# Second block's attention by pairs of heads, laid between the k-tiles of its projections

## The chip, the cores and the metric

The kernel runs on one core of a Trainium2 chip. The metric is the time of one execution in microseconds (us), median of 3 runs. The engines meet at semaphores: TensorE (PE in the rows, PEld its weight loads), VectorE (DVE), ScalarE (ACT), GpSimd (POOL) and SyncE (SP), which issues the weight transfers.

## The reference, cut to what matters

Two transformer blocks over 256 tokens of width 2048, in float32, one after the other. The change is in the attention half of the second:

```
u = rmsnorm_2(h, norm_attn[l])
p = jnp.split(u @ w_in[l], offsets, axis=-1)          # 2048 -> 4224 columns
o_mla = mla_mixer(...)   # 8 heads, latent q and kv, keys of 64+32, causal
o_fox = fox_mixer(...)   # 8 heads of 64, causal, forget-gate bias added to scores
o_nsa = nsa_mixer(...)   # 8 heads of 64 over 2 key groups: compressed, selected, window
o_swa = swa_mixer(...)   # 8 heads of 64 over 2 key groups, window 128, sinks
o = concatenate(...); o = rmsnorm_2(o per group of 512); h = h + o @ w_out[l]
```

Each attention is softmax(q k^T scale + bias) v. NSA's three branches are three softmaxes of the same queries, weighted by gates and added. The compressed branch has only 15 keys. An MLP follows (2048 to 8192 and back).

## The kernel before, in words

Activations lie transposed: 128 features on the partitions by 256 tokens, 16 k-tiles for 2048 features. A weight comes from memory in slots of 2048 columns (1 MB) into a ring of four (`ring`). ScalarE rounds each slot to a high part (`w_high`, L922) and VectorE subtracts to get the low part (`w_low`, L1394), both in two halves, into a pair of buffers. TensorE makes three products of high and low parts (float32r) for each k-tile: L484 to L486 where the weight is stationary ("wide"), L498 to L500 where the activation is ("tall"). Small products (queries from the latent, compression, scores, values) are plain float32 matmuls, which the trace records as two instructions each; transposes are recorded as one.

Every engine runs an order written out by hand. In the second block it is: the norm `attn2`; then the nine groups of `w_in_2` without a break (`group3` for `mla_c, fq, fk, fv, nq, nk, nv, sq`, then `small`), where the groups before `small` are 512 columns wide but for `nv` (384) and have four slots each; then, alone on TensorE, compression (L805, 64x64 pieces with 15 columns), the latent's norm (L652) and its products (L824, L830, L840, L492); then `attention("2")`; then the norm `group` and the product with `w_out_2`.

`attention("2")` runs 48 units, six for each of 8 heads: FOX, SWA, MLA, and NSA's three branches. For unit i TensorE does `score(i)` (L692, for FOX also L696 and L697 with 8 rows), then `turn(i-2)` (L711, three transposes) and `value(i-3)` (L722). VectorE scales the scores and adds the bias (L1501), takes the row maximum (L1512) and later divides by the row sum (L1535). ScalarE does the exponentials with their row sums (L1024), copies the turned probabilities out of PSUM (L1035) and the result (L1042). A head has 64 rows of contraction in its scores (96 in MLA) and 64 columns of output in its values, so one unit's matmuls use half of the array's rows or columns. The slots of `wout2` are split after the last unit.

SP's queue issues the slots in the order of `STREAM`. A slot is loaded again when its four-slots-older one is split, or, for a slot that TensorE reads raw, when its product is done.

## Time and profile before

| | us |
|---|---|
| median of 3 runs | 2594.13 |
| the runs | 2580.07 to 2596.78 |
| the profiled execution, its own time | 2572.51 |
| its span in the profile | 2570.3 |
| dense groups of `w_in_2` (in the span) | 1303 to 1494 |
| compression and latent products | 1494 to 1562 |
| `attention("2")` | 1562 to 1719 |
| norm `group` to the steady part of `wout2` | 1719 to 1745 |

Over the whole span TensorE is busy 94%, its weight loads 78%, VectorE 53%, ScalarE 38%. Matmuls overlap one another in the records, so the distance from start to start says what one costs, not its length. "PEclk" and the granted clock say which share of 2.4 GHz TensorE was given; it has two levels, 2.4 GHz (1.00) and 1.2 GHz (0.50), and a mean between them is a mix.

### The profile page before, as it was taken

What the parts mean: (1) busy time and instruction counts of PE and PEld (TensorE: products, weight loads), DVE (VectorE), ACT (ScalarE), POOL (GpSimd) and SP (SyncE); (2) the same over time, 40 slices, a digit from 0 to 9 for tenths busy, and PEclk for the clock granted to TensorE, in tenths of its full rate; (3) what the DMA queues carried; (4) which work ended last, traced back from release to release, by engine and by line L of the source; (5) the groups of instructions that cost most, each with busy time, mean ns of one, the idle gap of its engine ahead of it and who ended that gap; (6) DMA issues with size and microseconds to landing.
All of it is one profiled execution on the core that took longest, in us unless ns stands there. A gap on an engine that the chain in (4) does not pass through costs nothing.

```text
span 2570.3 us, 31240 instructions
## 1 busy us (share of the span) xinstructions
PE 2412.4 (94%) x12470; PEld 1998.0 (78%) x12470; DVE 1359.2 (53%) x1628; ACT 979.5 (38%) x1299; POOL 160.1 (6%) x61
## 2 busy tenths in 40 slices
PE   6988996998999999999989988979999999999997
PEld 5866565877888888888789975547888888888886
DVE  5388736464555554444554424665655555544444
ACT  4211105352434444444433424553534343444443
POOL 0388310000000000000000000000000000000000
PEclk9999998999999999999999977789999999999999
DMA  6433361549666655565535511004556665555552
GB/s 234 133 113 100 130 151 49 173 132 203 204 186 189 192 184 196 194 238 190 178 127 182 189 54 45 1 34 144 166 182 187 188 192 186 193 190 189 193 196 82
DMA packets 147777, 404.23 MB, mean 157 GB/s; under 512 B 14961, under 2 KB 22385, under 8 KB 126449
## 3 DMA queue, kind: packets, MB, share of 16 engines
q1 hardware_dynamic: 133056, 385.51, 45.5%
q10 hardware_dynamic: 14640, 17.61, 3.2%
q8 instruction: 56, 0.92, 0.1%
q14 instruction: 25, 0.20, 0.0%
HBM read 396.80 MB, written 6.29 MB: 157 GB/s over the span
## 4 chain that ended last, share of the span: by engine, by line
PE 83%; DVE 11%; ACT 3%; DMA 2%; issue 1%; ACTq 0%; DVEq 0%; SPq 0%
PE ps L569 17%; PE ps L605 11%; PE ps L607 11%; PE ps L606 11%; PE ps L570 9%; PE ps L476 3%; PE ps L492 2%; PE ps L484 2%; PE ps L486 2%; PE ps L485 2%; PE ps L692 2%; PE ps L722 2%; DVE scratch L1282 2%; DVE w_low L1394 2%; DMA raw_weights<-in_w_ff 1%; DVE scratch L1660 1%
## 5 line engine op out<-in xcount | busy, mean ns | idle before, releaser
L1394 DVE TENSOR_TENSOR w_low<-raw_weights,w_high 128x1024 fp32r<-128x1024 f32 (+1 forms) x660 | 776.3, 1218 | 902.1 <-ACT w_high L922 902.1
L922 ACT ACTIVATE w_high<-raw_weights 128x1024 fp32r<-128x1024 f32 (+1 forms) x660 | 660.4, 1049 | 900.5 <-PE ps L607 502.4
L569 PE MATMUL ps<-x_split,w_high 128*128 128x512 f32 x2048 | 719.9, 396 | 10.9 <-DVE w_low L1394 8.4
L570 PE MATMUL ps<-x_split,w_low 128*128 128x256 f32 x2048 | 573.8, 280 | 0.0
L605 PE MATMUL ps<-w_high,x_split 128*128 128x512 f32 x1280 | 499.9, 391 | 30.5 <-DVE x_split L1282 27.4
L606 PE MATMUL ps<-w_low,x_split 128*128 128x512 f32 x1280 | 499.1, 390 | 0.0
L607 PE MATMUL ps<-w_high,x_split 128*128 128x512 f32 x1280 | 499.0, 390 | 0.0
L569 PEld LDWEIGHTS ps<-x_split,w_high 128*128 128x128 f32 x2048 | 386.5, 189 | 101.3 <-DVE w_low L1394 8.4
L570 PEld LDWEIGHTS ps<-x_split,w_low 128*128 128x128 f32 x2048 | 389.2, 190 | 0.0
L605 PEld LDWEIGHTS ps<-w_high,x_split 128*128 128x128 f32 x1280 | 241.0, 188 | 82.1 <-DVE x_split L1282 28.1
L607 PEld LDWEIGHTS ps<-w_high,x_split 128*128 128x128 f32 x1280 | 240.9, 188 | 50.4
L606 PEld LDWEIGHTS ps<-w_low,x_split 128*128 128x128 f32 x1280 | 241.1, 188 | 49.9
L476 PE MATMUL ps<-x_over_high,raw_weights 128*128 128x256 f32 x768 | 170.0, 382 | 0.5
L476 PEld LDWEIGHTS ps<-x_over_high,raw_weights 128*128 128x128 f32 x768 | 145.4, 191 | 25.5 <-issue 3.3
L484 PE MATMUL ps<-x_split,w_high 128*128 128x256 f32 x416 | 118.8, 286 | 7.5 <-issue 7.2
L485 PE MATMUL ps<-x_split,w_high 128*128 128x256 f32 x416 | 118.6, 285 | 0.0
L486 PE MATMUL ps<-x_split,w_low 128*128 128x256 f32 x416 | 118.5, 285 | 0.0
L939 ACT ACTIVATE region<-ps 128x1024 f32<-128x1024 f32 (+4 forms) x20 | 18.0, 901 | 206.3 <-PE ps L476 111.1
L484 PEld LDWEIGHTS ps<-x_split,w_high 128*128 128x128 f32 x416 | 80.8, 194 | 8.1 <-issue 8.0
L1024 ACT ACTIVATE scratch<-scratch,small_stats 128x128 f32<-128x128 f32 (+2 forms) x120 | 52.3, 437 | 80.7 <-DVE small_stats L1512 64.9
L485 PEld LDWEIGHTS ps<-x_split,w_high 128*128 128x128 f32 x416 | 80.8, 194 | 0.0
L486 PEld LDWEIGHTS ps<-x_split,w_low 128*128 128x128 f32 x416 | 80.7, 194 | 0.0
(221 smaller groups left out, 2013.4 us busy)
## 6 DMA issues: line engine op xcount, KB each, us to landing
raw_weights<-in_w_ff SPq DMA_DIRECT2D x128, 1024.0 KB, 5.2
raw_weights<-in_w_up SPq DMA_DIRECT2D x64, 1024.0 KB, 5.3
raw_weights<-in_w_down SPq DMA_DIRECT2D x64, 1024.0 KB, 4.9
raw_weights<-in_w_in SPq DMA_DIRECT2D x62, 1024.0 KB, 5.4
raw_weights<-in_w_out SPq DMA_DIRECT2D x32, 1024.0 KB, 4.9
raw_weights<-in_w_mem_kv SPq DMA_DIRECT2D x8, 1024.0 KB, 7.3
t_table<-region ACTq DMA_DIRECT2D x1, 4096.0 KB, 46.0
region<-t_table ACTq DMA_DIRECT2D x1, 3072.0 KB, 18.0
```

Of the source, the lines that this page charges most:

```text
L476: last = nc.tensor.matmul(acc[:, c], w[:, P * c:P * c + P], x, start=(kt == 0 and c % 2 == 0), stop=(kt == kts - 1), skip_group_check=True)
L484: nc.tensor.matmul(o, h, xh_, start=(first and c % 2 == 0), stop=False, skip_group_check=True)
L485: nc.tensor.matmul(o, h, xl_, start=False, stop=False, skip_group_check=True)
L486: last = nc.tensor.matmul(o, wl[:, P * c:P * c + P], xh_, start=False, stop=done, skip_group_check=True)
L569: nc.tensor.matmul(o, wh[:, q, w], xs[:, kt], start=(kt == 0), stop=False, skip_group_check=True)
L570: last = nc.tensor.matmul(o[:, 0:S], wl[:, q, w], xh[:, kt], start=False, stop=(kt == KT - 1), skip_group_check=True)
L605: nc.tensor.matmul(o, h, wh[:, r], start=(first and j == 0), stop=False, skip_group_check=True)
L606: nc.tensor.matmul(o, h, wl[:, r], start=False, stop=False, skip_group_check=True)
L607: last = nc.tensor.matmul(o, l, wh[:, r], start=False, stop=True, skip_group_check=True)
L922: nc.scalar.activation(split_slot(wh_t, k)[:, r], ring_slot(n)[:, r], ACT.Copy).then_inc(rounded, 1)
L1024: last = nc.scalar.activation(s, s, ACT.Exp, bias=nmax[:, r, t:t + 1], accum_out=psumr[:, r, t:t + 1])
L1394: V.tensor_tensor(split_slot(wl_t, k)[:, r], ring_slot(n)[:, r], split_slot(wh_t, k)[:, r].bitcast(f32), ALU.subtract).then_inc(split_read ...
```

## The change

The order of the second block's attention half is rewritten on all engines.

- **Pairs.** The 48 units of one head become 24 duos of two heads (`duo`): 4 of MLA, 12 of NSA, 4 of SWA, 4 of FOX, in this order. The heads of a pair lie on different halves: `ACROSS` pairs a head of key group 0 with one of key group 1, so their scores contract over partitions 0 to 63 and 64 to 127; `EVEN` pairs an even head with an odd one. Values of the two go to output partitions 0 to 63 and 64 to 127. VectorE and ScalarE handle both heads in one instruction where shapes allow. NSA's branches no longer add up in PSUM: each is copied to `mix`, and VectorE adds them (`branches`).
- **Weaving.** `duo_step(p)` (values of p-3, turns of p-2, scores of p) is called between k-tiles of the last five groups: `sq`, `fq`, `fk`, `fva`, `fvb` (`fv` is cut into two groups of 256 columns). `WOVEN` says how many duos go to each slot: eight slots have two, eight have one. The latent's products are called between k-tiles of `nv`, compression between those of `nq`. Only the turns and values of the last duos stand after the last group.
- **Halves.** In the woven part ScalarE and VectorE split the next slot by halves, one half to a duo (both to one, where the slot has one). `wout2`'s first slots are split before the group norm.
- Groups, their slots and their PSUM buffers stand in a new order, `small` first; other buffers moved with them.

```diff
-W2_GROUPS = ("mla_c", "fq", "fk", "fv", "nq", "nk", "nv", "sq")
-STREAM += [(g, 4, True, 1) for g in W2_GROUPS]
-STREAM += [("small", 2, True, 1), ("cmpk", 1, False, 1), ("cmpk2", 0, False, 1), ("cmpv", 1, False, 1), ("cmpv2", 0, False, 1),
-           ("uqa", 1, False, 1), ("uqar", 0, False, 1), ("uqb", 1, False, 1), ("uqbr", 0, False, 1), ("kper", 0, False, 1),
-           ("kna", 0, False, 1), ("knb", 0, False, 1), ("mv", 1, False, 1),
+STREAM += [("small", 2, True, 0), ("mla_c", 4, True, 0), ("nk", 4, True, 0), ("uqa", 1, False, 0), ("uqb", 1, False, 0),
+           ("nv", 4, True, 0), ("ukv", 1, False, 0), ("cmpk", 1, False, 0), ("cmpv", 1, False, 0), ("nq", 4, True, 0),
...
+        EVEN = [(2 * i, 2 * i + 1) for i in range(4)]
+        ACROSS = [(0, 5), (1, 4), (2, 7), (3, 6)]
...
+        DENSE2 = ("small", "mla_c", "nk", "nv", "nq", "sq", "fq", "fk", "fva", "fvb")
+        WOVEN = {"sq": (2, 2, 1, 2), "fq": (2, 1, 2, 2), "fk": (1, 2, 2, 1), "fva": (1, 1), "fvb": (1, 1)}
+        WOVEN_SLOTS = [(g, j) for g in WOVEN for j in range(len(WOVEN[g]))]
+        AHEAD = WOVEN_SLOTS[1:] + [("wout2", 0)]
...
+            def duo_scores(p):
+                x = duos[p]
+                n = x["n"]
+                for t, _, w in KEYS2:
+                    w = min(w, n)
+                    o = [ps[:, 4 + a, n * t:n * t + w] for a in range(2)]
+                    for a in range(2):
+                        last = nc.tensor.matmul(o[a], x["q"][a][:, P * t:P * t + P], x["k"][a][:, 0:w], start=True, stop=not x["extra"])
+                    if x["extra"]:
+                        rows = [slice(64 * a, 64 * a + 8) for a in range(2)]
+                        col = [ident[64 * a:64 * a + 8, 64 * a + h:64 * a + h + 1] for a, h in enumerate(x["heads"])]
+                        for a in range(2):
+                            nc.tensor.matmul(o[a], fc8[rows[a], P * t:P * t + P], col[a].to_broadcast([8, w]), start=False, stop=False)
+                        for a in range(2):
+                            last = nc.tensor.matmul(o[a], col[a].to_broadcast([8, P]), fneg[rows[a], 0:w], start=False, stop=True)
+                m.did(last, "scores2", p)
+            def duo_turn(p):
+                x = duos[p]
+                n = x["n"]
+                w = min(P, n)
+                for a in range(2):
+                    for kt, t, c in turns_of(x):
+                        k0 = (KEYS2[t][1] if n == S else n * t) + P * kt
+                        last = nc.tensor.transpose(ps[0:w, 6 + a, c:c + P], prob2[:, p % 2, a, k0:k0 + w], ident[:, :])
+                m.did(last, "turned2", p)
+            def duo_value(p):
+                x = duos[p]
+                w = min(P, x["n"])
+                turns = turns_of(x)
+                for kt, t, c in turns:
+                    for a, h in enumerate(x["heads"]):
+                        o = ps[x["base"][a]:x["base"][a] + 64, 6 + t, 384:512]
+                        last = nc.tensor.matmul(o, x["v"](kt, h), probT2[0:w, a, c:c + P], start=(kt == 0),
+                                                stop=((kt + 1, t) not in [(u[0], u[1]) for u in turns]), skip_group_check=True)
+                m.did(last, "value2", p)
+            def duo_step(p):
+                if 0 < p < ND:
+                    pe.wait_ge(dve_done, at("scaled2", p - 1))
+                elif 0 <= p - 2 < ND:
+                    pe.wait_ge(dve_done, at("probs2", p - 2))
+                if p >= 4:
+                    pe.wait_ge(act_done, at("out2", p - 4))
+                elif p == 3:
+                    pe.wait_ge(act_done, at("probT2", 0))
+                if p >= 3 and p - 3 == ND - 1:
+                    pe.wait_ge(act_done, at("probT2", p - 3))
+                for first, group_name in ((SWA0, "sq"), (FOX0, "fk"), (FOX0 + 3, "fva"), (FOX0 + 5, "fvb")):
+                    if p == first:
+                        pe.wait_ge(act_done, at("evac", group_name))
+                if 0 <= p - 3 < ND:
+                    duo_value(p - 3)
+                if 0 <= p - 2 < ND:
+                    duo_turn(p - 2)
+                if p < ND:
+                    duo_scores(p)
...
+            def dense(name, form="wide", width=512, sk=SK, after=None):
+                b = DENSE2.index(name)
+                if b >= 2:
+                    pe.wait_ge(act_done, at("evac", DENSE2[b - 2]))
+                for j in range(KT // sk):
+                    k = SPLIT_OF[SLOT0[name] + j]
+                    wh, wl = (split_slot(t, k)[:, 0:sk * width].rearrange("p (k c) -> p k c", k=sk) for t in (wh_t, wl_t))
+                    for q in range(sk):
+                        kt = sk * j + q
+                        if q % (sk // 2) == 0:
+                            pe.wait_ge(split_ready, 2 * k + 1 + q // (sk // 2))
+                        if b == 0 and kt % 4 == 0:
+                            pe.wait_ge(dve_done, at("attn2", "out", kt // 4))
+                        a = (wh[:, q], wl[:, q], xh[:, kt], xl[:, kt], kt == 0, kt == KT - 1)
+                        last = wide3(pair4(b % 2), *a, cols=width // P) if form == "wide" else tall3(pair(b % 2), *a, n=width)
+                        if q == sk - 1:
+                            last.then_inc(split_used, 1)
+                        if after is not None:
+                            after(kt)
...
+            def latent(kt):
+                if kt == 0:
+                    pe.wait_ge(dve_done, at("mlan", "out"))
+                    pe.wait_ge(blk2_loaded, 80)
+                    queries(0)
+                if kt == 2:
+                    queries(1)
+                if kt == 4:
+                    queries_turned(0)
+                if kt == 6:
+                    queries_turned(1)
+                if kt == 8:
+                    keys(0)
+                if kt == 10:
+                    keys(1)
...
+            def compressed(kt):
+                if kt < 8:
+                    compress(kt // 4, kt % 4)
...
+            dense("small", width=256, sk=8)
+            dense("mla_c")
+            dense("nk", after=latent_sums)
+            dense("nv", "tall", 384, after=latent)
+            dense("nq", after=compressed)
             pe.wait_ge(dve_done, at("ready2"))
-            pe.wait_ge(act_done, at("evac", "mv"))
-            attention("2")
+            pe.wait_ge(act_done, at("evac", "cmpv2"))
+            for g in WOVEN:
+                def duos_after(kt, g=g):
+                    sk = KT // len(WOVEN[g])
+                    j, q = kt // sk, kt % sk
+                    ticks = TICKS[g, j]
+                    if len(ticks) == 2 and q in (0, 2):
+                        duo_step(ticks[q // 2])
+                    if len(ticks) == 1 and q == sk // 2 - 1:
+                        duo_step(ticks[0])
+                if g in ("fva", "fvb"):
+                    dense(g, "tall", 256, 8, after=duos_after)
+                else:
+                    dense(g, after=duos_after)
+            for p in range(TAIL0, ND + 3):
+                duo_step(p)
...
+            for (g, j), (nxt, q) in zip(WOVEN_SLOTS, AHEAD):
+                ticks = TICKS[g, j]
+                for c, p in enumerate(ticks):
+                    if c == 0 and j == 0 and g in DONE_BY:
+                        done = DONE_BY[g]
+                        if done == "fq":
+                            act.wait_ge(pe_done, at("scores2", NSA0 - 1))
+                        evac2(done, *homes[done])
+                    duo_back(p)
+                    for h in (c,) if len(ticks) == 2 else (0, 1):
+                        round_half(nxt, q, h)
+                    duo_exps(p)
...
+            def low_half(name, j, h):
+                n, k = SLOT0[name] + j, SPLIT0[name] + j
+                dve.wait_ge(rounded, 2 * k + h + 1)
+                r = slice(HALF * h, HALF * (h + 1))
+                V.tensor_tensor(split_slot(wl_t, k)[:, r], ring_slot(n)[:, r], split_slot(wh_t, k)[:, r].bitcast(f32),
+                                ALU.subtract).then_inc(split_ready, 1)
...
+            def duo_scale(p, negsink):
+                x, r = duos[p], p % 2
+                n = x["n"]
+                dve.wait_ge(pe_done, at("scores2", p))
+                m.own()
+                by_t = lambda a: a.rearrange("p (t k) -> p t k", k=n)
+                if n == S:
+                    for t, k0, w in KEYS2:
+                        ins = V.scalar_tensor_tensor(prob2[:, r, :, k0:k0 + w], ps[:, 4:6, S * t:S * t + w], x["scale"], x["biases"][t],
+                                                     ALU.mult, ALU.add)
+                        m.did(ins, "scaled2", p)
...
+            def duo_normal(p):
+                x, r = duos[p], p % 2
+                n = x["n"]
+                dve.wait_ge(act_done, at("exp2", p))
+                if x["sink"]:
+                    tt(psumr2[:, r], psumr2[:, r], esink2[:, r], ALU.add)
+                    m.own()
+                m.did(V.reciprocal(pinv2[:, r], psumr2[:, r]))
+                m.own()
+                if x["gate"] is not None:
+                    i, j = (8 + 3 * h + x["gate"] for h in x["heads"])
+                    tt(pinv2[:, r], pinv2[:, r], gates[:, :, i:j + 1:j - i], ALU.mult)
+                    m.own()
+                if n == S:
+                    for t, k0, w in KEYS2:
+                        e = prob2[:, r, :, k0:k0 + w]
+                        tt(e, e, pinv2[:, r, t].unsqueeze(2).to_broadcast([P, 2, w]), ALU.mult, "probs2", p)
...
+            for (g, j), (nxt, q) in zip(WOVEN_SLOTS, AHEAD):
+                ticks = TICKS[g, j]
+                for c, p in enumerate(ticks):
+                    duo_scale(p, rinv[:, S:S + 8])
+                    branches(p)
+                    for h in (c,) if len(ticks) == 2 else (0, 1):
+                        low_half(nxt, q, h)
+                    duo_normal(p)
```

On TensorE, in the first woven group but one step (program order; L539 to L541 are the three products of a k-tile's 128 columns, L811 values, L800 transposes, L782 scores). Before, where attention begins:

```order
L492 MATMUL ps<-raw_weights,mixed 128x512 x2
L849 MATMUL ps<-ident,region 128x32 x2
L692 MATMUL ps<-region 128x128
L696 MATMUL ps<-ident,region 128x128
L697 MATMUL ps<-region,ident 128x128
L692 MATMUL ps<-region 128x256
L696 MATMUL ps<-ident,region 128x256
L697 MATMUL ps<-region,ident 128x256
L692 MATMUL ps<-region 128x128
L692 MATMUL ps<-region 128x256
```

And now, at one of the first NSA duos:

```order
L541 MATMUL ps<-x_split,w_low 128x256
L811 MATMUL ps<-region 64x128 x6
L800 MATMUL ps<-ident,region 128x128 x6
L782 MATMUL ps<-region 128x128 x2
L782 MATMUL ps<-region 128x256 x2
L539 MATMUL ps<-x_split,w_high 128x256
L540 MATMUL ps<-x_split,w_high 128x256
L541 MATMUL ps<-x_split,w_low 128x256
```

Before, a unit follows a unit and no dense product stands near. Now a step of 12 + 4 program matmuls for two heads stands between k-tiles of 12 dense ones; two k-tiles (24 dense matmuls) lie between steps where a slot has two duos, four where it has one.

On VectorE, one unit before (L1501 scale, L1512 maximum, L1535 division):

```order
L1501 SCALAR_TENSOR_TENSOR scratch<-ps,region 128x128
L1501 SCALAR_TENSOR_TENSOR scratch<-ps,region 128x256
L1512 TENSOR_REDUCE small_stats<-scratch 128x1 x2
L1527 RECIPROCAL small_stats<-small_stats 128x2
L1282 TENSOR_TENSOR small_stats<-small_stats,region 128x2
L1535 TENSOR_SCALAR scratch<-scratch,small_stats 128x128
L1535 TENSOR_SCALAR scratch<-scratch,small_stats 128x256
```

One duo now (L1776 scale, L1787 maximum, L1764 half a slot's low part, L1521 division):

```order
L1776 SCALAR_TENSOR_TENSOR region<-ps,region 128x2x128
L1776 SCALAR_TENSOR_TENSOR region<-ps,region 128x2x256
L1787 TENSOR_REDUCE small_stats<-region 128x2 x2
L1764 TENSOR_TENSOR w_low<-raw_weights,w_high 128x1024
L1804 RECIPROCAL small_stats<-small_stats 128x4
L1521 TENSOR_TENSOR small_stats<-small_stats,region 128x4
L1521 TENSOR_TENSOR region<-region,small_stats 128x2x128
L1521 TENSOR_TENSOR region<-region,small_stats 128x2x256
```

The division of a duo now follows its own maximum, with half a slot between. Before, the next unit's scale and maximum came first: the reciprocal and what follows in the excerpt above belong to the unit before the one just scaled.

## Rows read from the trace of the kernel before

**Rows 1.** The page: span, busy time, granted clock in 40 slices of the span

```profile
span 2570.3 us, 31240 instructions
PE 2412.4 (94%) x12470; PEld 1998.0 (78%) x12470; DVE 1359.2 (53%) x1628; ACT 979.5 (38%) x1299; POOL 160.1 (6%) x61
...
PEclk9999998999999999999999977789999999999999
```

**Rows 2.** Windows: stretch, busy us (instructions) by engine, clock, DMA share, GB/s

```profile
1340.00:1360.00 20.00, 20.00 (x169) 20.00 (x169) 8.28 (x8) 9.15 (x10) 0.00 (x0) 1.00 0.55 176
1303.00:1494.00 191.00, 190.57 (x1441) 186.35 (x1441) 82.00 (x78) 74.54 (x84) 0.00 (x0) 0.99 0.54 170
1494.00:1523.00 29.00, 24.36 (x262) 23.70 (x262) 2.17 (x11) 4.64 (x16) 0.00 (x0) 0.58 0.12 34
1523.00:1562.00 39.00, 25.90 (x89) 15.51 (x90) 17.36 (x24) 16.41 (x26) 0.00 (x0) 0.88 0.25 91
1562.00:1719.00 157.00, 148.22 (x568) 87.68 (x568) 88.12 (x360) 76.28 (x281) 0.00 (x0) 0.74 0.01 2
```

**Rows 3.** Waits of 1562 to 1719: who for whom, us, times, longest

```profile
DVE scratch L1501 <- PE ps L692: 33.1, 31, 2.8
DVE scratch L1501 <- PE ps L697: 25.4, 8, 4.9
```

**Rows 4.** Windows within attention: busy TensorE at either clock

```profile
1585.80:1589.20 3.40, 3.40 (x10) 1.66 (x10) 2.02 (x8) 1.28 (x6) 0.00 (x0) 0.50 0.00 0
...
1616.40:1619.80 3.40, 3.40 (x19) 2.02 (x17) 2.23 (x10) 1.99 (x9) 0.00 (x0) 1.00 0.01 2
```

**Rows 5.** Timeline of TensorE in attention at full clock: start us, us, instruction

```profile
1597.45 0.92 PE L692 MATMUL ps<-region 64*128 64x128 f32 x4
1598.30 0.55 PE L711 MATMUL ps<-ident,scratch 128*128 128x128 f32 x3
1598.78 0.86 PE L722 MATMUL ps<-scratch,region 128*64 128x256 f32 x4
...
1602.46 0.49 PE L692 MATMUL ps<-region 64*128 64x128 f32 x2
...
1605.90 0.48 PE L711 MATMUL ps<-ident,scratch 128*128 128x128 f32 x1
```

**Rows 6.** Timeline of TensorE in the first block: tiles of 32 between projections

```profile
315.94 1.48 PE L675 MATMUL ps<-scratch,region 128*32 128x256 f32 x24
317.34 1.98 PE L492 MATMUL ps<-raw_weights,x_over_high 128*128 128x512 f32 x4
319.26 2.36 PE L666 MATMUL ps<-region 32*128 32x256 f32 x16
```

**Rows 7.** The chain of waits: float32 projection, and the splits before `moments`

```profile
87.27 27.63 PE ps L476 x128
...
1723.17 2.88 DVE w_low L1394 x3
```

**Rows 8.** Timeline of TensorE: compression begins

```profile
1493.99 9.65 PE L805 MATMUL ps<-region,raw_weights 64*64 64x15 f32 x128
```

**Rows 9.** Timeline of VectorE in one unit of attention

```profile
1627.47 0.62 DVE L1501 SCALAR_TENSOR_TENSOR scratch<-ps,region 128x128 f32<-128x128 f32 x2 [0.91 <-PE ps L692]
1628.12 0.61 DVE L1512 TENSOR_REDUCE small_stats<-scratch 128x1 f32<-128x128 f32 x2
...
1629.10 0.55 DVE L1535 TENSOR_SCALAR scratch<-scratch,small_stats 128x128 f32<-128x128 f32 x2
```

**Rows 10.** Timeline of ScalarE: a unit's two exponentials, then a copy

```profile
1625.74 0.40 ACT L1024 ACTIVATE scratch<-scratch,small_stats 128x128 f32<-128x128 f32 x1 [2.98 <-DVE small_stats L1512]
...
1626.63 0.36 ACT L1042 ACTIVATE mixed<-ps 64x256 f32<-64x256 f32 x1
1626.89 0.47 ACT L1035 ACTIVATE scratch<-ps 128x384 f32<-128x384 f32 x1
```

**Rows 11.** The page, costliest groups: the splits

```profile
L1394 DVE TENSOR_TENSOR w_low<-raw_weights,w_high 128x1024 fp32r<-128x1024 f32 (+1 forms) x660 | 776.3, 1218 | 902.1 <-ACT w_high L922 902.1
L922 ACT ACTIVATE w_high<-raw_weights 128x1024 fp32r<-128x1024 f32 (+1 forms) x660 | 660.4, 1049 | 900.5 <-PE ps L607 502.4
```

More of the change, by code:

```diff
@@ new lines, in compress @@
+            def compress(b, part):
+                name = ("cmpk", "cmpv")[b]
+                if part == 0:
+                    pe.wait_ge(dve_done, at("kcp", b))
+                    pe.wait_ge(act_done, at(*(("gates",) if b else ("evac", "mv"))))
+                w = raw(name).rearrange("p (l c) -> p l c", l=CMP_LEN)
+                for l in range(8 * part, 8 * part + 8):
+                    for g in range(2):
+                        r = slice(64 * g, 64 * g + 64)
+                        last = nc.tensor.matmul(pair(3 - b)[r, g, 0:NCMP], w[r, l], kcp[b][r, l], start=(l == 0), stop=(l == CMP_LEN - 1))
+                if part == 3:
+                    m.did(last, "slot", SLOT0[name])
+                    book["acc", name] = m.n
@@ L1718, in _ @@
             down("ff2_1", up("ff1_1", "mlp", t5_mask))
-            low("mla_c", 0)
+            low("small", 0)
             row_sums("mpost", "ff2_1")
```

645 lines of the change are left out of this document (351 added, 294 removed).

## The prediction

> **What bounds the kernel now.** I read the page first: TensorE is busy 94% of the span and the clock falls from 9 tenths to 7 only in four slices, about 1480 to 1735 us [rows 1]. The windows cut that region by stage [rows 2]. The dense groups run at clock 0.99 with TensorE never idle: 169 matmuls of 256 columns in 20 us, 118 ns each. Compression and latent products take 68 us (29 at clock 0.58, 39 with TensorE busy 25.90). Attention takes 157 us with TensorE busy 148.22, no weight loading, and a clock of 0.74. The waits say who ends last in attention: VectorE waits for scores 58.5 us in all [rows 3], so TensorE is the bound there, and it is slow for two reasons: each matmul uses half of the rows or columns, and the clock is at 1.2 GHz about half of the time. The second isn't idleness: two equal windows have TensorE busy 3.40 of 3.40 us, one at 0.50 and one at 1.00 [rows 4].
>
> The sum is made against the profiled execution, 2572.5 us (span 2570.3). The three timed runs stood 8 to 24 us above it (median 2594.1). I take 15 of that for the median.
>
> **The change, part by part.**
>
> *Compression and latent products* move between k-tiles of `nq` and `nv`. Nothing is removed, so their TensorE time at full clock remains: a 256-column float32 instruction costs 27.63/128 = 216 ns [rows 7], so queries 48 x 0.216 = 10.4, keys 16 x 0.216 = 3.5, sums 8 x 0.216 = 1.7, and 12 instructions of 512 columns (rotation, values) 12 x 0.43 = 5.2; the gates' transposes 0.5. Compression is 256 instructions at 9.65/128 = 75 ns [rows 8]; they now alternate between two quarters of the array. Bounds: 256 x 75 = 19 us if nothing overlaps, half of that, 10, if all does. I take 14. Sum 35. The stage cost 68, most of it chains of copy and wait that the k-tiles now cover: between two calls lie two k-tiles of `nv` or one of `nq`. Where cover fails: `nq`'s third and fourth slot can be loaded only when compression has read its two raw slots, and a load and a split then lie before k-tiles 8 and 12; and the last small chain (gelu, copy, `ready2`) ends about with `nq`. For this 4 us. Net 68 - 39 = **29 saved**.
>
> *Scores, transposes, values* per duo at full clock. In one unit, start to start: scores 0.85 (4 instructions), transposes 0.48 (3), values 0.80 to 0.86 [rows 5]. A pair's scores on different row halves: between 0.85 (both at once) and 1.7. Values, 12 instructions of 128 columns on different column halves: 0.8 to 1.6. Nearest rows: the first block's tiles of 32 columns run 24 instructions of 256 columns in 1.40 us, 58 ns each against 216 for a full one, and its tiles of 32 rows 16 in 2.43 us, 152 ns, with two in a row on the same rows [rows 6]. So overlap is real here; I take 0.9 and 0.8. Transposes use the whole array: 0.96 for six. NSA's two full branches and SWA: 2.7 us a duo, 12 duos, 32. MLA contracts over 96 rows, so its scores don't pair: 1.7 + 0.96 + 0.8 = 3.4, 4 duos, 14. FOX's scores take 3.44 in one unit (1602.46 to 1605.90 [rows 5]); as a pair the same again: 5.2, 4 duos, 21. The compressed branch 1.6 (bounds 1 to 2.5), 4 duos, 6. Together 73.
>
> *In and out of dense work.* Not in attention's rows. After 32-column tiles four 512-column instructions take 1.92 us from start to start (317.34 to 319.26 [rows 6]) against 4 x 0.43: 0.2 us. 24 steps x 0.2 = 5. The Trainium skill, "TensorEngine Tiling (Array Packing)", section Key Properties, speaks against the change here: a change of tiling mode drains the array. No row shows a drain longer than this 0.2 us; by the rule alone I could give no other price.
>
> *VectorE and ScalarE* in the woven part. A duo's scale, maximum and division each handle 768 elements in two instructions. One unit's 384 take 0.62, 0.61 and 0.55 [rows 9]; with 0.93 ns per further element (from 1218 ns for 1024 [rows 11]) 0.98 each. Two exponentials take 0.89 from start to start, four 1.8 [rows 10]. VectorE now waits for a duo's exponentials before it divides, so its cycle is 1.0 + 1.0 + 1.8 + reciprocal and gate 0.3 + 1.0 + handoffs 0.3 = 5.4 us; half a slot's low part, 1.22 [rows 11], lies inside the 1.8, and ScalarE's copies and rounding (0.8 + 0.4 + 1.05) inside VectorE's 3.3. Sinks add 0.9, the compressed branch needs 3.8. TensorE in a slot with two duos needs two k-tiles, 24 x 0.118 = 2.8, and a step of 2.7 + 0.2: 5.7 per duo. In a slot with one duo TensorE needs 5.7 + 2.9 = 8.6. So TensorE stays the bound by little; for SWA's three duos in shared slots and for jitter 6 us.
>
> *Tail.* After the last scores come scale, exponentials and division (5 us), turn, copy, values, copy (2.6), partly under the last four k-tiles: 2 us beyond TensorE's own work.
>
> *The rest.* `fv` as two groups: 192 instructions at 118 ns, 22.7, for 96 of 512 columns, 20.6: +2. The first slots of `wout2` are split earlier, so VectorE needn't do three halves (2.88 [rows 7]) before the group norm: -3. SP's queue has 16 woven slots in about 170 us and is no bound. The first block and the MLPs keep their order.
>
> Attention: 157 before, 73 + 5 + 6 + 2 = 86 now, **71 saved**. Sum: -29 - 71 + 2 - 3 = -101, 2472 for a profiled execution. With 15: **2487**, which I round to 2485 for the median. This holds if the clock in the woven part stays near 1.00: a step of 2.7 us lies beside at least 2.8 us of full-array work, which by itself ran at 0.99 to 1.00 [rows 2]. TensorE's work from 1303 to the end of attention is then 191 + 2 + 35 + 78 = 306 of 318 us.
>
> **Rivals.**
>
> *A, pairs don't overlap* (the change doesn't do what it says). Then 12 duos lose 0.8 in scores, FOX 3.4 each, 24 duos about 0.75 in values: 10 + 14 + 18 = 42, so 2527. Against it: the 58 ns. For it: the 152 ns of row tiles is only part of the way. 0.12.
>
> *B, VectorE's cycle binds.* The two-head division multiplies by a spread-out operand that no row here has, and handoffs may be longer. 16 duos in shared slots at 6.9 instead of 5.7 us give 19 more: 2505. For it: 5.4 against 5.7 is a thin margin. 0.15.
>
> *C, the clock sags.* If the woven part is granted 0.74, as attention was, its 91 dense + 78 us take 59 more: 2544. For it: half the array's work in a step is of the kind that ran at 0.50 [rows 4]; against it: first-block weaving of the same kind of tiles [rows 6] lies in slices of 9 tenths. The Trainium skill, "TensorE: Matmul & The Clock Gate", section Why this matters for your kernels, asks only that TensorE be kept busy without gaps; by that the woven part would run at full clock, the forecast. The trace speaks against the rule as it stands, since a fully busy window had 0.50 [rows 4]. 0.09.
>
> *D, slower.* The same mechanism to its end: small tiles in each step hold the whole woven part at 1.2 GHz, dense matmuls too. It costs 169 more, 68 above before: about 2655. It decides from a clock of 169/(169 + 101) = 0.63 on; below that the change loses. 0.03.
>
> *E, better.* Compression overlaps fully and the transposes cost less: 20 less, 2465. 0.04.
>
> **Chances and range.** The forecast has 0.54, its own range 2465 to 2510. All but D are faster by over 1% (1% is about what a measurement of this kernel can tell from no change; it is 26 us). I leave 0.03 for a sum that fails in a way I don't see and ends near zero: faster 0.94, same 0.03, slower 0.03. The range takes in A and B and half of the runs' scatter on each side: 2450 to 2530.
>
> **What the profile after would show.** From the first dense matmul (1303) to the last values 305 to 325 us (416 before), clock at least 0.95 from 1303 on. Duos: scores of an NSA pair in 0.9 us, FOX's in 3.5, values in 0.8; twice that is A. Steps start 5.7 us apart in shared slots and TensorE waits for VectorE under 10 us in all; waits of 15 to 30 us on the scale are B. Windows at 0.50 among the duos are C. `nq` longer than 40 us says the raw slots were under-priced. The forecast is wrong if TensorE's idle time or its time at 1.2 GHz in the woven part passes 15 us.

## The result, and the profile after

The change ran at 2475.75 us (median of four runs, 2472.41 to 2479.97), the kernel before beside it at 2588.02 (four, 2580.07 to 2596.78): a ratio of 0.957, 95% interval 0.954 to 0.961, or 112 us. The profiled execution took 2472.41 us.

The page of the changed kernel, to be held against [rows 1]: TensorE's busy share is the same 94%, but the four slices at clock 7 are gone, and VectorE has 152 instructions fewer (1476 for 1628) at nearly the same busy time.

```profile
span 2470.6 us, 31199 instructions
PE 2330.5 (94%) x12662; PEld 1955.9 (79%) x12662; DVE 1347.0 (55%) x1476; ACT 966.9 (39%) x1250; POOL 162.2 (7%) x61
...
PEclk9999999899999999999999999989999999999999
```

The windows by stage, TensorE only, answer to [rows 2]: stretch, its length, TensorE busy us (instructions), clock, DMA share, GB/s. In order they are: `small` and `mla_c`; `nk`; `nv` with the latent products; `nq` with the compression; `sq` and `fq` with their duos; `fk`; the two halves of `fv`; the tail of three steps.

```profile
1303.00:1341.00 38.00, 38.00 (x305) 0.95 0.48 147
1341.00:1365.40 24.40, 24.07 (x192) 1.00 0.28 89
1365.40:1401.00 35.60, 35.60 (x169) 1.00 0.48 163
1401.00:1437.50 36.50, 34.81 (x461) 1.00 0.51 180
1437.50:1515.00 77.50, 77.25 (x682) 1.00 0.35 113
1515.00:1555.00 40.00, 38.84 (x344) 1.00 0.35 106
1555.00:1602.00 47.00, 44.30 (x358) 0.93 0.27 90
1602.00:1610.00 8.00, 4.67 (x53) 1.00 0.44 131
```

From the first dense matmul (1302.54) to the end of the last values (1609.6) it is 307 us, where before it was 415 (1303.18 to 1718.3). Below, a stretch is measured from that first matmul to the start of the last values (306.2 us here) or to the first matmul of `wout2` (330.8), because the first matmul itself falls between 1302.5 and 1318.7 us from run to run, with nothing changed ahead of it.

A step of an NSA duo on TensorE's timeline (start us, us, instruction), to be held against [rows 5], where the scores of one head took as long as those of this pair:

```profile
1517.95 0.88 PE L811 MATMUL ps<-region 128*64 128x128 f32 x12
1518.76 0.87 PE L800 MATMUL ps<-ident,region 128*128 128x128 f32 x6
1519.56 0.93 PE L782 MATMUL ps<-region 64*128 64x128 f32 x8
```

From the start of one row to the start of the next: values 0.80 to 0.81, transposes 0.80, scores 0.85 to 0.86. A FOX duo's scores follow in six parts, 2.77 us for two heads, where [rows 5] had 3.44 for one unit (whose last two parts lay at a lower clock; see the section on the prediction):

```profile
1564.12 0.49 PE L782 MATMUL ps<-region 64*128 64x128 f32 x4
1564.55 0.49 PE L787 MATMUL ps<-ident,rinv 8*128 8x128 f32 x4
1564.87 0.39 PE L789 MATMUL ps<-rinv,ident 8*128 8x128 f32 x4
1565.19 0.70 PE L782 MATMUL ps<-region 64*128 64x256 f32 x4
1565.82 0.70 PE L787 MATMUL ps<-ident,rinv 8*128 8x256 f32 x4
1566.36 0.59 PE L789 MATMUL ps<-rinv,ident 8*128 8x256 f32 x4
1566.89 0.38 PE L553 MATMUL ps<-w_high,x_split 128*128 128x256 f32 x1
```

The waits of the woven stretch (1436 to 1605; who for whom, us, times, longest) answer to [rows 3]. VectorE still waits for scores, 37 us in all, and TensorE's only long wait is one for a split:

```profile
DVE region L1776 <- PE ps L789: 23.8, 4, 7.8
DVE region L1776 <- PE ps L782: 13.0, 7, 3.8
...
PE ps L553 <- DVE w_low L1764: 3.6, 4, 2.8
```

### The profile page after: what moved, and what is told of

Its sections match the earlier page's. It is cut to its first block, busy times and chain, and to the rows that moved or that the text cites. A ratio compares the mean times of both kernels' runs of the same rounds, so it can differ in the third digit from the quotient of the medians.

```text
span 2470.6 us, 31199 instructions
## 1 busy us (share of the span) xinstructions
PE 2330.5 (94%) x12662; PEld 1955.9 (79%) x12662; DVE 1347.0 (55%) x1476; ACT 966.9 (39%) x1250; POOL 162.2 (7%) x61
## 4 chain that ended last, share of the span: by engine, by line
PE 81%; DVE 12%; ACT 3%; DMA 2%; issue 1%; ACTq 0%; DVEq 0%; SPq 0%
PE ps L624 18%; PE ps L660 12%; PE ps L661 11%; PE ps L662 11%; PE ps L625 9%; PE ps L531 3%; PE ps L547 2%; DVE scratch L1521 2%; PE ps L539 2%; DVE w_low L1633 2%; PE ps L540 2%; PE ps L541 2%; DMA raw_weights<-in_w_ff 1%; DVE scratch L1947 1%; DVE mixed L1521 1%; PE ps L707 1%
## 5 line engine op out<-in xcount | busy, mean ns | idle before, releaser
L1633 DVE TENSOR_TENSOR w_low<-raw_weights,w_high 128x1024 fp32r<-128x1024 f32 (+1 forms) x628 | 738.5, 1218 | 860.0 <-ACT w_high L1096 860.0
L1096 ACT ACTIVATE w_high<-raw_weights 128x1024 fp32r<-128x1024 f32 (+1 forms) x628 | 628.9, 1049 | 864.6 <-PE ps L662 504.1
L539 PE MATMUL ps<-x_split,w_high 128*128 128x256 f32 x416 | 122.7, 295 | 9.8 <-DVE x_split L1521 7.3
L541 PE MATMUL ps<-x_split,w_low 128*128 128x256 f32 x416 | 118.3, 284 | 0.0
L539 PEld LDWEIGHTS ps<-x_split,w_high 128*128 128x128 f32 x416 | 80.4, 193 | 15.6 <-issue 11.8
L1113 ACT ACTIVATE region<-ps 128x1024 f32<-128x1024 f32 x10 | 10.2, 1023 | 180.4 <-PE ps L531 112.4
L541 PEld LDWEIGHTS ps<-x_split,w_low 128*128 128x128 f32 x416 | 80.5, 193 | 0.0
L1123 ACT ACTIVATE region<-ps 128x1024 f32 (+1 forms) x32 | 32.8, 1026 | 109.0 <-PE ps L625 109.0
```

Of the source, the lines that this page charges most:

```text
L539: nc.tensor.matmul(o, h, xh_, start=(first and c % 2 == 0), stop=False, skip_group_check=True)
L541: last = nc.tensor.matmul(o, wl[:, P * c:P * c + P], xh_, start=False, stop=done, skip_group_check=True)
L1096: nc.scalar.activation(split_slot(wh_t, k)[:, r], ring_slot(n)[:, r], ACT.Copy).then_inc(rounded, 1)
L1633: V.tensor_tensor(split_slot(wl_t, k)[:, r], ring_slot(n)[:, r], split_slot(wh_t, k)[:, r].bitcast(f32), ALU.subtract).then_inc(split_read ...
```

## The experiments

Each kernel is the change with one edit unless it says more; medians stand beside 2475.75, stretches (to the last values, to `wout2`) beside 306.2 and 330.8.

**Order of the heads.** Scores and values head by head; everything else alike:

```diff
-                for kt, t, c in turns:
-                    for a, h in enumerate(x["heads"]):
+                for a, h in enumerate(x["heads"]):
+                    for kt, t, c in turns:
```

> Each duo's scores and values are issued head by head instead of alternating between the two halves of the array; same instructions, same places. If neighbouring matmuls on different halves run at once (the forecast's price), alternation is what gives it: scores of a full NSA or SWA duo go from 0.9 to about 1.3 us, FOX's from 2.9 to 5.8, values from 0.8 to 1.4; 12 x 1.0 + 4 x 3.5 + 8 x 0.5 = about 30 us more than the changed kernel (2475 to about 2505). If the two halves hardly overlap and the pace is set by something per instruction (weight loads), less than 5 us more.

Measured: 2504.91 (2501.05 to 2509.74), ratio to before 0.968 [0.966, 0.971]; 29 us above the change, and 23 in the stretch to `wout2` (354.2). Where it went is not where I had put it. The values rose from 0.80 to 1.07 (start to start), but NSA's scores kept their time, 0.87:

```profile
1510.62 1.15 PE L809 MATMUL ps<-region 128*64 128x128 f32 x12
...
1512.50 0.93 PE L784 MATMUL ps<-region 64*128 64x128 f32 x8
```

FOX's scores doubled. One head's six parts now take 2.74 us, as long as both heads' did:

```profile
1607.02 0.48 PE L784 MATMUL ps<-region 64*128 64x128 f32 x2
1607.44 0.48 PE L786 MATMUL ps<-ident,rinv 8*128 8x128 f32 x2
1607.76 0.38 PE L787 MATMUL ps<-rinv,ident 8*128 8x128 f32 x2
1608.07 0.70 PE L784 MATMUL ps<-region 64*128 64x256 f32 x2
1608.70 0.70 PE L786 MATMUL ps<-ident,rinv 8*128 8x256 f32 x2
1609.24 0.59 PE L787 MATMUL ps<-rinv,ident 8*128 8x256 f32 x2
1609.76 0.48 PE L784 MATMUL ps<-region 64*128 64x128 f32 x2
```

So at full clock alternating is worth 4 x 2.7 = 11 us in FOX's four duos and 20 x 0.27 = 5 in the values, and nothing in NSA's scores. The k-tiles between the FOX steps also took 7.4 to 8.3 us instead of 6.4 to 6.5, and that is the clock. From the k-tiles before the first FOX duo to the last values it was granted 0.81 with TensorE hardly ever idle:

```profile
1568.00:1640.00 72.00, 69.22 (x396) 0.81 0.21 74
```

Half of full clock was granted for 27 us among the duos, against 7 in the change. By that an estimate: (27 - 7) / 2 = 10 us of the difference are the clock. With the 16 above it is 26; about 2 come back because TensorE waits less for splits (5.3 us of idle time among the duos against 7.1), and 23 were measured.

That left open whether NSA's halves work beside each other at all.

**Both heads on one half of the rows.**

```diff
-                        last = nc.tensor.matmul(o[a], x["q"][a][:, P * t:P * t + P], x["k"][a][:, 0:w], ...)
+                        b = a if p < NSA0 else 0
+                        last = nc.tensor.matmul(o[a], x["q"][b][:, P * t:P * t + P], x["k"][b][:, 0:w], ...)
...
-                        rows = [slice(64 * a, 64 * a + 8) for a in range(2)]
-                        col = [ident[64 * a:64 * a + 8, 64 * a + h:64 * a + h + 1] for a, h in enumerate(x["heads"])]
+                        rows = [slice(0, 8)] * 2
+                        col = [ident[0:8, h:h + 1] for h in x["heads"]]
```

> In the scores of the NSA, SWA and FOX duos both heads take the queries, keys and eight-row gate operands of the duo's first head, so that both lie on the same half of the rows; the order still alternates between them, and their sums go to the same two banks as before. The second head's scores are left out (it gets the first one's). MLA, transposes and values are as in the change. Theory (the halves of the rows work beside each other, whichever order they are issued in): NSA and SWA scores rise from 0.86 to 1.1 to 1.5 us, FOX scores from 2.94 to 5 or more; with four NSA/SWA compressed duos, twelve full ones and four FOX duos that is 12 to 20 us, median 2488 to 2496. Rival (0.86 us is what 64 rows cost anyway, and only the order of the eight-row products counts): NSA and SWA scores stay at 0.86, FOX at 3, the median within 3 us of 2476.

Measured: 2493.18 (2489.14 to 2500.32), ratio 0.964 [0.961, 0.968]; +17, stretch +21 (327.3). The timeline shows NSA's scores at 1.50, and those of FOX at 4.8 to 4.9 (here one of its parts with 256 keys, 0.98 against 0.54 from start to start):

```profile
1472.95 1.57 PE L783 MATMUL ps<-region 64*128 64x128 f32 x8
...
1593.33 1.13 PE L788 MATMUL ps<-ident,rinv 8*128 8x256 f32 x4
```

The halves do work beside each other. Of the 21 us the scores explain about 18 (12 full duos by 0.65, 4 compressed by 0.44, 4 of FOX by 2.1); the clock, at half for 20 us among the duos instead of 7, by the same estimate as above about 7, less some shorter waits. In NSA's scores, two matmuls a head, the order doesn't matter; in FOX's, six matmuls a head, it decides. Which property of FOX's does it isn't shown: its runs are longer, but they also go back and forth between operands of 64 and of 8 rows, and head by head they do so twice as often, each part taking the same time for one head as for two. No run tells the two apart. The Trainium skill, "TensorEngine Tiling (Array Packing)", Overview, gives up to 2 times for a contraction of 64 or less; here it was 1.50/0.86 = 1.75. Against MLA's scores, which contract over 96 rows and take 1.12 us for the same number and width of matmuls, the pair's 0.86 is 1.3 times faster.

**Duos behind the groups.** Four MLA duos stay in `sq`; the other 20 run after the last dense product, with ScalarE's and VectorE's orders to match:

```diff
-        WOVEN = {"sq": (2, 2, 1, 2), "fq": (2, 1, 2, 2), "fk": (1, 2, 2, 1), "fva": (1, 1), "fvb": (1, 1)}
+        WOVEN = {"sq": (1, 1, 1, 1), "fq": (0, 0, 0, 0), "fk": (0, 0, 0, 0), "fva": (0, 0), "fvb": (0, 0)}
```

> Pairs as in the changed kernel, but only the 4 MLA duos stand between k-tiles (of sq); the other 20 run after the last group with nothing beside them. If weaving carries most of the gain: alone, a duo takes the cycle scale, maximum, exponentials, division of 5.4 us (3.8 compressed, 6.3 SWA), 104 us for 20, where they cost TensorE about 60 between k-tiles; so 45 to 65 us more than the changed kernel (about 2520 to 2540), and the clock falls among them as it did before. If pairing carries it, under 15 us more (2490) and the clock stays at 1.00.

Measured: 2531.38 (2527.61 to 2538.58), ratio 0.979 [0.976, 0.982]; +56, the stretch to `wout2` 387.7, +57. The 20 duos alone take 127 us, of which TensorE is idle 41, mostly waiting for VectorE's scale (L1778; for the compressed duos another 7.5 us at L1783), and its clock averages 0.70 (first the window: busy us of TensorE, its weight loads, VectorE, ScalarE and GpSimd, then clock, DMA share, GB/s; then the waits):

```profile
1543.00:1670.00 127.00, 85.99 (x610) 61.14 (x608) 68.06 (x182) 62.90 (x221) 0.00 (x0) 0.70 0.04 16
```

```profile
PE ps L811 <- DVE region L1778: 27.6, 15, 3.6
```

So of the change's 112 us about half is the weaving of those 20 duos, as cover for the softmax and for the clock together.

**Latent products in one piece**, behind the first k-tile of `nv`:

```diff
-                if kt == 2:
+                if kt == 0:
...
-                if kt == 14:
+                if kt == 0:
```

> All products of the latent stand behind the first k-tile of nv instead of one after every second k-tile; ScalarE's and VectorE's orders follow. If the k-tiles between them cover the chains of copy, rotation and copy: 12 to 20 us more (before, the same products and their sums took 39 us of which TensorE was busy 26, at 0.88). If those chains were short anyway and only the order of loads mattered, under 5 us more.

Measured: 2486.51 (2484.16 to 2486.93), ratio 0.961 [0.958, 0.963]; +11, to `wout2` 337.2, +6.4: under the 12 to 20 that I had expected, and 4 of the median's 11 lie outside the stretch. The same products take 24 us in a row against 18 spread. 2.5 of the 6 are one wait for weights, and about 2 are the clock, at half for 3.4 us there (1390.12 to 1393.53). TensorE never waited for a copy or a rotation between them, so the k-tiles cover less of such chains than I had thought; probably the order in which the products now stand does the rest, which no run shows alone.

**Whole slots for the first duo**: the split of the coming slot isn't shared between its two duos.

```diff
-                    for h in (c,) if len(ticks) == 2 else (0, 1):
+                    for h in (0, 1) if c == 0 else ():
```

> In slots with two duos both halves of the next slot's split go to the first duo, none to the second. Theory: VectorE's 1.22 us too much lies where it waits 1.8 us for exponentials, 0.6 us over in 8 slots, and TensorE is the bound: 0 to 5 us more than the changed kernel. Rival (the halves carry the weaving): 10 us or more.

Measured: 2477.13 (2465.81 to 2484.86), ratio 0.957 [0.953, 0.961]; stretch to `wout2` 330.8, the change's own. Halving the splits brings nothing by itself.

**More work for one engine at a time.** Twice the maxima on VectorE, then twice the transposes on TensorE:

```diff
+                    for again in range(2):
-                    for t, k0, w in KEYS2:
-                        m.did(V.tensor_reduce(nmax2[:, r, t], prob2[:, r, :, k0:k0 + w], AX.X, ALU.max, negate=True), "max2", p)
+                        for t, k0, w in KEYS2:
+                            m.did(V.tensor_reduce(nmax2[:, r, t], prob2[:, r, :, k0:k0 + w], AX.X, ALU.max, negate=True), "max2", p)
+                        m.own()
```

> The row maxima of the 20 full duos are taken twice on VectorE, about 1.0 us more on its cycle for each duo, 20 us of VectorE work in all. Theory (TensorE bounds the woven stretch, VectorE and ScalarE have room): first dense product to last values stays near 307 us, at most 6 us more, and most of that where the feed-forward split of a slot is already late; the median stays within 6 us of the change's 2476. Rival B of the prediction (VectorE's cycle is the bound, or nearly): each duo's extra 1.0 us shows in full, 15 to 20 us, median 2491 to 2496.

```diff
-                for a in range(2):
+                for a in (0, 1, 0, 1):
                     for kt, t, c in turns_of(x):
```

> Each duo's transposes are done twice on TensorE, 0.80 us more for each of 20 full duos and 0.54 for the four compressed ones: 18 us of TensorE work. Theory (TensorE bounds the stretch): all of it shows, 16 to 20 us, median 2492 to 2496, first dense to last values 323 to 327 us. Rival (the wait for VectorE or ScalarE ends last at each step, TensorE has slack): under 6 us.

Measured: the maxima cost 14 us (2489.91, 2485.94 to 2495.16; ratio 0.961 [0.959, 0.964]), stretch +15.2 for 24 us more on VectorE (busy 1371.1 against 1347.0). The transposes cost 18 us (2493.45, 2482.89 to 2496.80; 0.964 [0.962, 0.966]), stretch +13.7; a step's transposes took 1.46 to 1.53 instead of 0.80, some 15 us in all. So nearly all of TensorE's addition shows, as the theory had it (the median within its 2492 to 2496, the stretch 3 under its 323). But 15 of VectorE's 24 us show too, which I had put at 6 at most; on that the theory was wrong, and the rival's rise (15 to 20 us) is the one that the stretch shows, though the median lies 1 us under its range. The waits of the kernel with double maxima (1446 to 1633) say where: mostly at the low halves of the coming weights, and only 3 us at the scale.

```profile
PE ps L553 <- DVE w_low L1764: 8.4, 3, 5.6
PE ps L539 <- DVE w_low L1764: 6.2, 6, 2.3
```

Both engines are near their limit: TensorE is the bound by little, and VectorE reaches it through the splits that stand in its queue behind a duo's scale and maximum.

**The one long wait.** In the change TensorE stood still for long only once among the duos, before the first k-tile of `fva`; VectorE's timeline shows the sums of the three branches (L1521 on `mixed`) ahead of the split:

```profile
1552.96 1.01 DVE L1787 TENSOR_REDUCE small_stats<-region 128x2 f32<-128x256 f32 x2
...
1554.28 1.33 DVE L1521 TENSOR_TENSOR mixed<-mixed 128x256 f32<-128x256 f32 x3
1555.54 2.35 DVE L1764 TENSOR_TENSOR w_low<-raw_weights,w_high 128x1024 fp32r<-128x1024 f32 x2
```

TensorE's side, and the two windows behind it: the clock stays at half for all of the first and for 0.9 us of the second, 5.9 us in all.

```profile
1556.89 0.55 PE L553 MATMUL ps<-w_high,x_split 128*128 128x256 f32 x1 [2.82 <-DVE w_low L1764]
```

```profile
1556.90:1561.90 5.00, 5.00 (x23) 5.00 (x24) 2.26 (x5) 0.60 (x1) 0.00 (x0) 0.50 0.55 188
1561.90:1566.90 5.00, 5.00 (x46) 3.48 (x44) 0.00 (x0) 2.62 (x5) 0.00 (x0) 0.91 0.07 25
```

The edit:

```diff
                     duo_scale(p, rinv[:, S:S + 8])
-                    branches(p)
                     for h in (c,) if len(ticks) == 2 else (0, 1):
                         low_half(nxt, q, h)
                     duo_normal(p)
+                    branches(p)
```

> Only VectorE's order in a step changes: the sums of the three branches come after the low halves of the split and the division, not before them. Theory (the 3 us stop between the last k-tile of fk and the first of fva, and the half clock behind it, come from the branch sums of the last SWA duo standing ahead of the low halves): the stop goes, 3 to 5 us less, median 2471 to 2473. Rival (the clock falls there for another reason, or the maxima and the sinks alone make the halves late): within 2 us of the change.

Measured: 2472.85 (2463.49 to 2490.41), ratio 0.956 [0.953, 0.959]: 3 us, less than the medians' scatter. The stretch to `wout2` is 328.0 (-2.9), that to the last values 304.7 (-1.5), and it is 10.7 instead of 14.0 us from the last SWA duo's scores to the first FOX duo's. The wait stays (sinks and maxima alone make the halves late), yet shorter by 0.7, and behind it the clock is 1.00 at once:

```profile
1558.20 0.35 PE L553 MATMUL ps<-w_high,x_split 128*128 128x256 f32 x1 [2.10 <-DVE w_low L1764]
```

```profile
1558.20:1563.20 5.00, 5.00 (x46) 4.48 (x46) 3.63 (x8) 2.26 (x8) 0.00 (x0) 1.00 0.56 192
```

So most of the gain at this place, 3.3 us, is the clock, not the wait. It doesn't all last: at 1598.60 this kernel is granted half clock for 3.4 us with TensorE busy throughout, where the change has full clock, and about half of the 3.3 is lost. Behind the last values 1.4 us come back in the group norm's 32 sums, which ran at full clock here, as they did before the change; in the change they took 8.55 us:

```profile
1611.38 7.17 PE L707 MATMUL ps<-region,ones 128*128 128x256 f32 x32 [1.57 <-ACT region L1047]
```

Nothing in the edit touches these sums. I had expected the wait itself to go; that was wrong, and of the 2.9 us to `wout2` the edit can claim about 1.5.

**Towards a better version.** Four edits together (the late branch sums, and the three below; ScalarE's order follows, with the second split of `wout2` behind the squares), and then the same without the fourth:

```diff
-                if kt < 8:
-                    compress(kt // 4, kt % 4)
+                if kt < 4:
+                    compress(kt // 2, 2 * (kt % 2))
+                    compress(kt // 2, 2 * (kt % 2) + 1)
...
-        WOVEN = {..., "fva": (1, 1), "fvb": (1, 1)}
+        WOVEN = {..., "fva": (1, 2), "fvb": (1, 1)}
...
-            for p in range(TAIL0, ND + 3):
-                duo_step(p)
-            norm("group", xo, [(0, 4), (4, 4), (8, 4), (12, 4)])
+            group_sums(0)
+            duo_step(ND + 1)
+            group_sums(2)
+            group_sums(3)
+            duo_step(ND + 2)
+            group_sums(1)
```

> A version meant to beat both, four edits in one: branch sums late as above (-3 to -5); the compression's 64 matmuls of 32 positions in the first four k-tiles of nq instead of eight (-2 to -3, raw slots free earlier); a second FOX duo in the second slot of fva, so that one of the three steps behind the last dense product comes before its end (-2 to -4); the squares and sums of three of the four norm groups before the last steps instead of behind them (-4 to -6). In all 8 to 15 us under the change, median 2461 to 2468. If these stretches are covered by something else, or the sums merely move on TensorE without filling its waits, 0 to 5 us.

> As e8_best, but all squares and sums of the group norm stay behind the last values, as in the change. Theory (the early sums fill waits of TensorE): first dense product to the first matmul of wout2 2 to 4 us longer than e8's 324.7. Rival (run at half clock between the last steps, the early sums cost what they save behind): within 1 us of 324.7.

Measured: 2471.44 (2459.70 to 2476.38), ratio 0.953 [0.951, 0.956], stretch to `wout2` 324.7 (-6.2); without the early sums 2470.68 (2465.86 to 2483.59), 0.955 [0.953, 0.958], stretch 327.0. The packed compression brings 2.8 us (the first duo's scores start 133.2 us after the first dense matmul, not 136.0). Without the early sums the last values start 5.7 us earlier than in the change (300.5): 2.8 from the compression, 1.5 as in the kernel with late branches, and most of the rest goes with the second FOX duo in one slot, for the wait before the next-to-last values is 0.78 us, not 1.76. Of the 5.7 `wout2` sees 3.8: the sums wait longer for ScalarE's squares (2.37 against 1.57), and they run at half clock for most of their time:

```profile
1620.77 9.67 PE L707 MATMUL ps<-region,ones 128*128 128x256 f32 x32 [2.37 <-ACT region L1048]
```

At full clock they take 7.17, and these 2.5 us are as much as the whole difference between the two versions, 2.4, which by itself lies in the 2 to 4 that the theory gave. So that the early sums gain anything but the clock isn't shown, nor whether they keep the clock up or it fell by chance. Both versions beat the kernel before clearly; against the change the stretch with all four edits is 6 us better, under the 8 to 15 expected, and the medians (-4, intervals that overlap) can't tell it from no change. In the version with all four, norm sums now stand where TensorE waited for the last softmax and copies. But 16 of them take 3.5 us (1620.52 to 1624.07), where the wait that they fill was 1.17.

```profile
1620.52 3.62 PE L715 MATMUL ps<-region,ones 128*128 128x256 f32 x16
1624.07 0.88 PE L820 MATMUL ps<-region 128*64 128x128 f32 x12
```

## Why the prediction was right, step by step

*The bound.* Right. TensorE stays the bound, VectorE waits for it, and the four slices at clock 7 are gone. That the margin is thin (5.4 against 5.7 us, rival B) was right too: doubling the maxima made most of B's price appear.

*Latent products and compression* were over-priced, 39 us against about 30. The queries (4.99 each), rotations, keys and values came as the rows said; compression took eight times 1.04, 8.3 us, not 14: below even my lower bound of 10. The bounds were wrong, because I read [rows 8] as full clock. That row runs from 1493.99 to 1503.6, and the clock there is 1.00 only until 1498.6, then 0.50. At 1.00 the instructions start 56 ns apart (36 in the first 2.01 us), not 75:

```profile
1493.99:1496.00 2.01, 2.01 (x36) 1.00 0.00 0
```

By that 256 instructions cost 14 us with no overlap at all and 7 with all of it; 33 ns each, as measured, are 1.7 times faster, near what the pairs of scores gained and not beyond a halving. My 14 was the price of no overlap by accident. `nq` took 36 us of at most 40, with one wait of 1.7. One of the eight calls:

```profile
1403.12 1.11 PE L991 MATMUL ps<-mixed,raw_weights 64*64 64x15 f32 x32
```

*Scores, transposes, values.* Values 0.81 for 0.8, NSA's scores 0.86 for 0.9: the two prices nearest to a row. MLA's scores were 1.12, not 1.7, FOX's 2.77, not 3.44, and transposes 0.80, not 0.96. FOX's error is again a row read at the wrong clock: I took all of it as full clock, but its last two parts lay at 0.58, and at full clock one head's six parts take 2.74 us (in the kernel by heads).

```profile
1604.14:1605.90 1.76, 1.76 (x6) 0.58 0.00 0
```

MLA's and the transposes' prices are times of short groups of 64 rows or three instructions, taken twice; eight instructions of 96 rows, and six transposes, cost less than that. Together 65 us, not 73. Rival A (no overlap) has fallen: taking the overlap away in the experiments cost 17 and 29 us, some 7 and 10 of it, by the estimates above, by way of the clock.

*In and out.* Two k-tiles between steps take 3.05 us for 24 matmuls of 118 ns, 2.83: 0.2 a step, as taken. No drain beyond it shows.

*Waits* were put at 6 and came to 4.1 plus about 3 for the 5.9 us at half clock. *Tail:* 2 foreseen; the waits in it are 1.76 and 1.17. *Clock:* 0.93 and up in every window of the woven part (0.95 was foretold), so C and D fell. The 5.9 us after 1556.89 are the place where it showed.

*Group norm* was the step that failed. I took off 3 us because three splits no longer stand before `moments`. From the last values to the first matmul of `wout2` it is 23.8 us (1609.6 to 1633.4) against 23.0 before (1718.3 to 1741.3). VectorE now waits 10.70 us there for TensorE's 32 sums, 8.55 us at clock 0.84. Before, the splits had lain beside these sums, 7.17 us at full clock, and ended 1.2 us behind them, so they had cost hardly more than 1 us. In the three variants whose sums also ran at full clock (double maxima, late branches, same half) the way from the start of the last values to `wout2` is 23.3 us, against 23.9 before. So at full clock the change gains 0.6 us here, not 3, and the half clock in the sums took 1.4.

```profile
1619.76 1.42 DVE L1612 TENSOR_SCALAR rinv<-ps 128x256 f32<-128x256 f32 x4 [10.70 <-PE ps L707]
```

*The sum.* The stretch came to 307, not 318 (the 416 before, less 29 and 71, and 2 more). Products and compression were 9 under their price and attention about 6 (80 for 86); 4 of these 15 were lost again in the dense k-tiles, and only the window at clock 0.95 up to 1341 shows a part of them, about 2; the other 2 I can't place. The group norm came 4 worse than put (2.4 for the splits, 1.4 for the clock), and from `wout2` to the end it was 837.2 us against 829.0 before, 8 more for work that the change doesn't touch. So the profiled 2472.4 meets the forecast 2472 because errors of opposite sign cancel: that it fits to a microsecond is luck, that the bound, the overlap and the cover were right is not. The median lies 3 us above the profiled execution, not 15: that surcharge, read from three runs of before of which the profiled one was the quickest, was the term most in error. It was 12 too much; rounding 2487 down to 2485 took 2 of them back, and the rest are the 9 us between 2485 and 2476.

## What to carry to other kernels

Look up the granted clock of every row before taking a price from it: two of the prices here came from rows that lay partly at half clock. Alternate the heads of a pair from matmul to matmul. Head by head, two matmuls of scores overlapped as well, three of values took a third longer, and FOX's chains of six didn't overlap at all; whether the length of the run does it or FOX's mix of 64 and 8 rows isn't shown. Weave latency-bound softmax steps between dense k-tiles so that TensorE hardly waits and seldom drops its clock, and look in the other engine's queue for what stands ahead of the dense stream's own splits: that is where its lack of room appears first. An operation taken off an engine before a wait saves little if another engine's work of the same length lies beside it.

## What the runs showed that I had not expected

The length of a stop doesn't tell whether the clock falls behind it. A still TensorE of 2.82 us, before `fva`, was followed by 5.9 us at half clock, and one of 2.10 us at the same place (late branches) by none. But shorter ones there were followed by 3.4 us at half clock: 2.01 us in the kernel by heads, and 1.96 in that with both heads on one half:

```profile
1570.68 0.35 PE L553 MATMUL ps<-w_high,x_split 128*128 128x256 f32 x1 [1.96 <-DVE w_low L1765]
...
1571.20:1574.50 3.30, 3.30 (x18) 0.50 0.47 144
```

The Trainium skill, "TensorE: Matmul & The Clock Gate", section Why this matters for your kernels, puts drops of the clock down to idle gaps. These stops are at most a part of it: [rows 4] had half clock without any gap, and so had the kernel with late branches at 1598.60 and the kernel by heads for 6.8 us from 1578.31, among FOX's duos. What decides is open.

The feed-forward's up projection has two speeds, with the clock at 1.00 and TensorE busy throughout either time: 568 or 579 matmuls in 100 us. Here is one window of it in the second block of the change, and one of the kernel with double transposes:

```profile
1873.00:1973.00 100.00, 100.00 (x568) 1.00 0.61 183
```

```profile
1890.00:1990.00 100.00, 100.00 (x579) 1.00 0.63 190
```

In all eleven profiled executions of the changed kernel and its variants the stretch from `wout2` to the end goes with this rate: 831.3 to 831.9 us in the four at 579, 836.8 to 837.7 in the seven at 568. The profiled execution of before was at 578 and took 829.0. In the first block three of the eleven had the slower rate (the latent cluster and both of the last versions), with the second block's independent of it. So about 6 of the 8 us above are this, and it is probably part of the scatter of the medians. What sets the rate stays open.
